# HGRN sample outputs with the query as 32-column stationary operand, norm squares in column groups and row scales from 128 rows, in a two-layer retention and HGRN2 step

## The reference

```python
# HGRN2, one sample token (b) and head (h); state S is 128 x 128
S_new = diag(f) @ S + outer(1 - f, i)
o     = S_new.T @ q
on    = o * rsqrt(mean(o*o) + 1e-6) * norm_g          # over the 128 values of a head
out   = (silu(g) * on) @ w_out
# retention, per head of 512 values
on    = (o - mean(o)) * rsqrt(var(o) + 1e-5) * gn_g
```

## Time and profile before

| | us |
|---|---|
| median of 3 runs | 1637.79 (1637.14 to 1643.33) |
| profiled execution | 1640.53, span 1638.7 |
| TensorE busy in the span | 1597.8 |
| VectorE busy | 621.6 |
| ScalarE busy | 421.6 |
| GpSimd busy | 79.4 |

### The profile page before, as it was taken

How to read it: one execution, slowest core, us unless ns; L and a number is a source line. 1 busy time by engine, 2 the same in 40 slices (tenths; PEclk the granted TensorE clock), 3 DMA queues, 4 the chain that set the end, 5 groups by cost and what they waited for, 6 DMA issues and landing times.

```text
span 1638.7 us, 32102 instructions
## 1 busy us (share of the span) xinstructions
PE 1597.8 (98%) x14348; PEld 955.6 (58%) x14348; DVE 621.6 (38%) x934; ACT 421.6 (26%) x606; POOL 79.4 (5%) x106
## 2 busy tenths in 40 slices
PE   7999999999999999999999999999999999999997
PEld 7888887999999999873333333333333333333333
DVE  6566576566655889543011100100111001001114
ACT  4444544444455575631001000010010000100001
POOL 1122221000000011001000000000000000000001
PEclk9999999999999999998999999999999999999999
DMA  9678879546455455267999999999999999999994
GB/s 337 223 270 294 296 259 383 168 155 197 132 179 192 164 167 168 96 260 298 398 411 393 423 417 391 420 417 388 420 383 422 416 385 422 417 389 421 403 404 191
DMA packets 138232, 514.93 MB, mean 314 GB/s; under 512 B 6700, under 2 KB 61172, under 8 KB 129780
## 3 DMA queue, kind: packets, MB, share of 16 engines
q1 hardware_dynamic: 117780, 447.93, 70.6%
q0 software_dynamic: 15824, 57.97, 10.1%
q10 hardware_dynamic: 4496, 7.02, 1.3%
HBM read 472.43 MB, written 40.47 MB: 313 GB/s over the span
## 4 chain that ended last, share of the span: by engine, by line
PE 86%; DVE 6%; DMA 2%; issue 1%; ACT 1%; POOL 0%; DVEq 0%; ACTq 0%
PE ps L1879 84%; DMA ring<-in_moe_w_up 2%; DVE ring_low_parts L1317 1%; DVE ring L1366 1%; PE ps L2025 1%; DMA ring<-in_state_retention 1%; ACT ring_low_parts L965 1%; DVE ring L1620 0%; DVE ring L1592 0%; DVE arena L1544 0%; DVE ring L1593 0%; ACT ring L1088 0%; DVE expert_arena L1846 0%; PE ps L2129 0%; DVE expert_arena L1836 0%
## 5 line engine op out<-in xcount | busy, mean ns | idle before, releaser
L1879 PE MATMUL ps<-ring,expert_x_turned 128*32 128x448 f32 x5376 | 510.0, 540 | 2.2 <-DMA ring<-in_moe_w_up 2.2
L1879 PEld LDWEIGHTS ps<-ring,expert_x_turned 128*32 128x32 f32 x5376 | 175.9, 110 | 333.7 <-issue 333.7
L1879 PE MATMUL ps<-normed_high,ring_low_parts 128*128 128x264 f32 x1344 | 268.8, 291 | 6.9 <-DVE arena L1312 3.0
L1879 PE MATMUL ps<-ring,expert_hidden_turned 128*32 128x512 f32 x2496 | 269.3, 592 | 0.0
L965 ACT CAST ring_low_parts<-ring 128x1024 fp32r<-128x1024 f32 (+2 forms) x180 | 180.0, 1001 | 245.9 <-PE ps L1879 241.6
L1317 DVE TENSOR_TENSOR ring_low_parts<-ring,ring_low_parts 128x1024 fp32r<-128x1024 f32 (+2 forms) x180 | 208.0, 1163 | 81.2 <-ACT ring_low_parts L965 81.2
L1879 PEld LDWEIGHTS ps<-normed_high,ring_low_parts 128*128 128x128 f32 x1344 | 218.4, 191 | 8.7 <-issue 3.6
L1811 DVE TENSOR_TENSOR expert_arena<-expert_arena,ps 128x1344 f32<-128x1344 f32 x16 | 24.9, 1554 | 510.8 <-PE ps L1879 510.8
L1879 PEld LDWEIGHTS ps<-ring,expert_hidden_turned 128*32 128x32 f32 x2496 | 83.3, 110 | 183.7 <-issue 183.4
L1879 PE MATMUL ps<-normed_low,ring_low_parts 128*128 128x264 f32 x640 | 161.6, 287 | 0.0
L1879 PE MATMUL ps<-h_parts,ring_low_parts 128*128 128x264 f32 x1056 | 130.0, 285 | 0.2 <-DVE h_parts L1301 0.2
(11 more groups left out here) (285 smaller groups left out, 1250.8 us busy)
## 6 DMA issues: line engine op xcount, KB each, us to landing
ring<-in_moe_w_gate SPq DMA_DIRECT2D x64, 1792.0 KB, 18.4
ring<-in_moe_w_down SPq DMA_DIRECT2D x48, 2048.0 KB, 22.7
ring<-in_moe_w_up SPq DMA_DIRECT2D x48, 1792.0 KB, 19.4
expert_piece_slot<-in_moe_w_up SPq DMA_DIRECT2D x16, 1792.0 KB, 19.9
ring<-in_ret_w_in SPq DMA_DIRECT2D x8, 2048.0 KB, 12.5
ring<-in_state_retention POOLq DMA_DIRECT2D x32, 512.0 KB, 7.8
out_ret_s<-ring POOLq DMA_DIRECT2D x32, 512.0 KB, 4.9
ring<-in_hg_w_in SPq DMA_DIRECT2D x8, 2048.0 KB, 8.2
```

What stands on the lines that cost most here:

```text
L1879: return nc.tensor.matmul(out, lhsT, rhs, start=first, stop=last)
```

## The change

The sample outputs of head t-2 exchange their operands: the query of a sample is the stationary operand, as one column of a 128x32 block that is otherwise zero, and the updated state is the moving one, with 128 columns. The outputs are rows now. Sample b goes to column group b % 4 (partitions 32c to 32c+31 of the bank), row b // 4. The padded queries (`hq_pad`, two buffers) are cleared once by GpSimd and filled by one VectorE copy per head ahead of `update_head`. ScalarE copies 128 columns instead of 8 to `s_rows`. After tile 10 a new step, `sample_rows`, turns the rows back: 8 matmuls, one for each head, with the rows of a head (128x128) as stationary operand and `hsel` (8 columns) as moving one, into a new group `("srow", 0)` in bank 0; ScalarE copies it out at t = 11.

The sums of squares go to partitions 32 (h % 4) of their bank: in retention each head in its own column group, in HGRN heads in turn over the four groups. Root and reciprocal run over 128 partitions, and the selecting matrix `rowsel` has 128 rows, zero but for one.

```diff
-    put("col_hg", np.broadcast_to(np.eye(8) / P, (P, 8, 8)).astype(f))
-    put("rowsel", np.broadcast_to(np.eye(8)[:, :, None], (8, 8, P)).astype(f))
+    put("col_hg", np.broadcast_to(np.eye(2, 32) / P, (P, 2, 32)).astype(f))
+    for j in range(8):
+        hs[32 * (j % 4) + j // 4, j] = 1
+        rs[32 * (j % 4) + j // 4, j] = 1
...
+        if t == 10:
+            add((("srow", 0), 0))
...  # GpSimd, after the retention layer
+            nc.gpsimd.memset(hq_pad, 0.0).then_inc(hq_zero, 1)
...  # ScalarE
-                        d = A.copy(oH[:, t - 2, NP_:NT], o[:, 256:264])
+                        d = A.copy(s_rows[:, t - 2, :], o[:, 256:384])
                     frees(d, ("itr", t - 1))
+                if t == 11:
+                    filled(act, ("srow", 0))
+                    frees(A.copy(oH[:, :, NP_:NT], bank(("srow", 0))[:, 0:64].rearrange("p (h b) -> p h b", h=8)), ("srow", 0))
...
-                    freed(act, ("itr", 8))
+                    freed(act, ("srow", 0))
...
-                    frees(A.activation(std8, bank(("hvar", 0), 8)[:, 0:NT], ACT.Sqrt, bias=eps_n[0:8]), ("hvar", 0))
+                    frees(A.activation(std8, bank(("hvar", 0))[:, 0:NT], ACT.Sqrt, bias=eps_n), ("hvar", 0))
...  # VectorE
                 if 1 <= t <= 8:
+                    if t >= 3:
+                        filled(dve, ("itr", t - 2))
+                    else:
+                        dve.wait_ge(hq_zero, 1)
+                    V.tensor_copy(hq_pad[:, (t - 1) % 2, :, 0], hq[:, t - 1, NP_:NT]).then_inc(hq_pad_ok, 1)
                     update_head(t - 1)
...  # TensorE, retention
-                    i = mm(bank(("var", 0), 8)[:, 0:NT], col_gn[:, h, :], square_of(h, e), h + e == 0, h + e == 6)
+                    i = mm(ps[32 * h:32 * h + 32, FILL[("var", 0)][0], 0:NT], col_gn[:, 0, :], square_of(h, e), e == 0, e == 3)
...
-                close(mm(bank(("rs", h))[:, 0:NT], rowsel[0:8, h, :], rstd[0:8, :]), ("rs", h))
+                close(mm(bank(("rs", h))[:, 0:NT], rowsel[:, h, :], rstd[:, :]), ("rs", h))
...  # TensorE, rows_of_i
                     freed(pe, ("ib", 1, h - 1))
+                    pe.wait_ge(hq_pad_ok, h)
+                    q = hq_pad[:, (h - 1) % 2, :, :].rearrange("p b n -> p (b n)")
                     for b in range(NS):
-                        i = mm(o[:, 256 + b:257 + b], hunit[(h - 1) % HUNITS][:, b, :], hq[:, h - 1, NP_ + b:NP_ + b + 1])
+                        c, a = b % 4, 32 * b - b // 4
+                        i = mm(ps[32 * c:32 * c + 32, FILL[("itr", h)][0], 256:384], q[:, a:a + 32],
+                               hunit[(h - 1) % HUNITS][:, b, :], b < 4, b >= 4)
                 close(i, ("itr", h))
+
+            def sample_rows():
+
+                freed(pe, ("itr", 8))
+                claim(("srow", 0))
+                for h in range(HH):
+                    i = mm(bank(("srow", 0))[:, NS * h:NS * h + NS], s_rows[:, h, :], cc("hsel"))
+                close(i, ("srow", 0))
...  # head_squares
-                    i = mm(bank(("hvar", 0), 8)[:, 0:NT], col_hg[:, h, :], osq[:, h, :], h == 0, h == 7)
+                    c = h % 4
+                    i = mm(ps[32 * c:32 * c + 32, FILL[("hvar", 0)][0], 0:NT], col_hg[:, h // 4, :], osq[:, h, :], h < 4, h >= 4)
...  # the loop over t
                 if 1 <= t <= 9:
                     rows_of_i(t)
+                if t == 10:
+                    sample_rows()
...
-                close(mm(bank(("hrs", h))[:, 0:NT], rowsel[0:8, h, :], rstd8), ("hrs", h))
+                close(mm(bank(("hrs", h))[:, 0:NT], rowsel[:, h, :], rstd8), ("hrs", h))
```

More of the change, by code:

```diff
@@ L422, in hybrid_step @@
         table_mark = part(small, 318, 2)
-        std8 = arena[0:8, 13568:13568 + NT]
-        rstd8 = arena[0:8, 13568 + NT:13568 + 2 * NT]
+        std8 = arena[:, 13568:13568 + NT]
+        rstd8 = arena[:, 13568 + NT:13568 + 2 * NT]
+        hq_pad = part(ring, spare + 1024, 2, 8, 32)
+        s_rows = part(arena, 6336 + 1088, 8, P)
         oH = hk
@@ L1046, in _ @@
             filled(act, ("var", 0))
-            frees(A.activation(std[0:8, :], bank(("var", 0), 8)[:, 0:NT], ACT.Sqrt, bias=eps_g[0:8]), ("var", 0))
+            frees(A.activation(std[:, :], bank(("var", 0))[:, 0:NT], ACT.Sqrt, bias=eps_g), ("var", 0))
             for h in range(RH):
@@ L1468, in _ @@
             freed(dve, ("var", 0))
[L1469 removed]
+            V.reciprocal(rstd[:, :], std[:, :]).then_inc(r8_ok, 1)
             for h in range(RH + 1):
```

15 lines of the change are left out of this document (10 added, 5 removed).

## The result

| | before | after |
|---|---|---|
| median of 6 runs each, us | 1637.47 (1636.08 to 1643.33) | 1628.70 (1627.38 to 1630.80) |
| profiled execution, span, us | 1640.53, 1638.7 | 1628.0, 1626.2 |

The ratio is 0.9943 (95% interval 0.9924 to 0.9963). The kernel became 8.8 us faster; the forecast was 1.0 us and its range ended at 1632.5. The profiled spans lie 12.5 us apart, more than the medians, because the profiled run of before was one of its slower ones. Three executions of two later kernels ran at a granted clock of 0.742 to 0.849 and took 1815 to 2058 us; they are left out of all medians here. First the page of after, then what answers to the rows of before.

The account below looks back on a forecast made before the run. More than half the span is the expert loop, paced by TensorE. Terms: +1.1 tile 10, -2.5+0.2 squares, -0.3 retention, +0.5 clock = -1.0, giving 1639.5 us profiled, 1636.8 on the median; range 1632.5 to 1642.5.

Parts of the forecast that it names:

- no gain is larger than the shift: Expert stage: a shift ahead of it is handed on one for one, and gains cannot exceed that shift.
- Sample outputs, TensorE: HGRN sample matmuls: 1.70 us a head becomes 0.8, saving 7.2 in all; tiling-mode drains could make the sum 0.6 worse.
- What VectorE lets through: 583 to 657 us: 3.6 us of cast waits recovered, less added copies; VectorE 2.8 us earlier, bounds 0 and 4.1.
- Tile 10: sample_rows waits for VectorE's scaling, TensorE idles some 3 us; product 8 starts 1.1 later, a clock fall adds 1.7.
- Norm squares: HGRN squares over four column groups: 3.65 us becomes 1.1, saving 2.5, with 0.2 given back.
- Retention: Retention norm squares, a head's four matmuls in one column group: 0.3 us saved, bounds 0 and 0.7.
- The clock behind the scale matmuls: After the HGRN scale matmuls the 6.5 us fall to 0.50 goes, worth 1.2 us, bounds 0 and 2.7.
- The clock elsewhere: Other clock falls: the one at 641.2 us worth nothing either way, the one at 265.8 going only in a rival.
- the end does not follow the start: Sign of a wrong prediction: the expert stage's start moves and its end does not move with it.
- A: Column groups do not overlap at 128 columns or drains eat it, leaving the tile 10 claim: +6, 1644 us; chance 0.2.
- B: Clock falls at 696 and 265.8 us both go and no new one comes: -4.4, 1633.4 us; chance 0.15.
- C: TensorE's saving counts in full because VectorE's order is looser: -8.3, 1629.5 us; chance 0.05.

Follow-up runs that it names:

- norm part alone: Kernel before with only the changed norms (column-group squares, 128-partition roots, 128-row scales), sample outputs as before, the eight new constant columns kept: 1621.95 us.
- rows in bank 2: Changed kernel with sample_rows put in bank 2 instead of bank 0, so it need not wait for the scaling of tile 10: 1621.78 us.
- same pair at 37376: The norm part alone and the changed kernel with rows in bank 2, both with the ring at byte 37376: 1623.65 and 1620.30 us.
- before shifted: Kernel before with two more keep_busy matmuls of 512 columns ahead of the routing stage: 1638.31 us.
- sample part alone: Kernel before with only the new sample outputs (padded queries, column groups, sample_rows at tile 10), norms made as before: 1633.19 us.
- retention norm alone: Kernel before with only the retention norm changed, HGRN norm and sample outputs as before, ring unmoved: 1636.16 us.

## Why the prediction was wrong, point by point

**The step that failed.** The prediction took the change to consist of its instructions alone: "no gain is larger than the shift" ahead of the experts, and no term at all for the eight new constants of `hsel`. They move the ring of weights, and that is worth 7.1 us in the changed kernel (1635.76 without, 1628.70 with). Without it the time lies inside the range of 1632.5 to 1642.5. Two more terms were wrong and hide each other: the fall of the clock at tile 10, and the falls behind 702 us.

**Sample outputs, TensorE: right.** 0.7 us a head, forecast 0.8. The Trainium skill's rule on changing the tiling mode (TensorEngine Tiling (Array Packing), Key Properties) says that each change drains TensorE. By the 228 ns of a record of 264 columns, four records of 128 columns one after another take 0.44 us; that is an estimate of the streaming alone, with the four groups fully overlapped. The 0.58 us to the next start leave 0.14 for the change behind, and 0.1 stands ahead: about 0.25 us for both, not the 0.3 each that would have made the sum worse. (The 0.50 of the prediction was half of a row that held such a change itself, so it was not streaming alone.)

**What VectorE lets through: right.** The waits for the cast went from 4.1 to 0.4 us (forecast 3.6 recovered). Where the claim was out of the way, the scale matmuls started 4.3 us earlier than in the norm part alone (683.12 against 687.43). But the two profiles were already 1.0 us apart at the reciprocal ahead of the HGRN layer, first with the rows in bank 2, then the norm part alone:

```profile
519.60 1.80 DVE L1324 RECIPROCAL rstd<-std 128x264 f32<-128x264 f32 x1 [1.71 <-ACT std L969]
```

```profile
520.60 1.80 DVE L1319 RECIPROCAL rstd<-std 128x264 f32<-128x264 f32 x1 [1.72 <-ACT std L967]
```

So 3.3 us belong to the sample outputs, and the same pair at 37376 gives 3.3 as well (4.69 less 1.43). The forecast was 2.8, with bounds 0 and 4.1.

**Tile 10: the mechanism was right, the term mis-sized.** It was claimed that TensorE would idle some 3 us for the scaling (3.90) and that the clock would fall (it did). The sum had 1.1 for the start of product 8 and 1.7 for the clock, 2.8 in all. Measured against the norm part alone, product 8 starts 2.3 later (657.77 against 655.45) and takes 2.6 more (6.22 for 3.6): 4.95 us, and the squares start 4.98 later. What was mis-sized is the fall: it was to be 3.4 us long, like the one at 641; it was 10.3 us, and took in `sample_rows` as well (1.65 us of the 2.3). Its length is a matter of the run: with the same wait it was 6.8 us in the changed kernel with the ring moved on, where the squares start 3.9 us later than in the norm part with the ring not moved (686.44 against 682.57). By medians the whole sample part cost 6.7 us beside the norm part, 5.8 with the ring at a slow place, and 3.1 beside the old norms (1633.19 against 1630.04).

**Norm squares: right.** 1.10 us, and from the first square to the scale matmuls 9.68 us became 6.96: 2.7 saved, forecast 2.5 less 0.2. **Retention: low.** Forecast 0.3 of a bound of 0.7; in the profile of the kernel with that norm alone the reciprocal starts 0.6 us earlier (258.05 for 258.64). That is one pair of profiles; in kernels whose retention norm is that of before the start lies anywhere from 258.64 to 260.54 at this place of the ring, later where the clock had fallen near 220 us.

**The clock behind the scale matmuls: the fall went, and was worth what was said.** In the kernels with 8 rows the fall behind them is there each time, 6.8 us long (before, before shifted, before with the ring moved, sample part alone, retention norm alone). In the twelve with 128 rows it is gone in ten, and two have one of 3.4 us up to 8 us behind (after with the ring moved, norm part with the ring at 36928). From the first output tile to the selection it takes 39.23 us after and 40.18 before: 0.95 us, forecast 1.2. That 128 rows in place of 8 take it away is shown by the kernel that changes only this, as far as one profile can; it is worth no more than 1.5 us in the median. In retention the same swap did not take the fall away: behind the scale matmuls from 8 rows there were 6.8 us at the lower clock in five profiles and 3.4 in one, behind those from 128 rows 6.8 in five, 3.4 in five and none in one.

**The clock elsewhere: a missed term.** The sum went through the falls at 265, 641 and 696 us and stopped at 702. The longest of all, 17.1 us at 0.50 in the routing, was in the same trace, at 736.6 to 753.7. The prediction treated everything behind the HGRN layer as one block that is shifted. It is not one: in the 17 profiles the way from selection to experts takes 8.9 us with no fall, 10.4 to 10.6 with one of 3.4, 11.7 with one of 6.8, and 15.3 and 16.6 with those of 13.7 and 17.1. By all runs the norm part lowers what the clock withholds from 19.5 to 9.3 us (ring unmoved). Over 99 runs of before the time follows the clock: 51 runs with a mean granted clock of 0.988 or more had a median of 1634.8 us, the 48 others 1642.1. So the norm part's 8.6 us are about 3.3 from the instructions (2.7 and 0.6, each from one pair of profiles), and the rest goes with a higher granted clock. This account does not close: 3.3 and 10.2 make 13.5, 4.9 more than the 8.6, and of these 3.2 went into longer waits for weights in the profile. Why the runs of the norm part meet fewer falls is open. Of the ten kernels with both new norms eight have no fall in the routing of their profile, of the seven others one has none; but each norm alone does not do it (6.8 us with the HGRN norm, none with the retention norm), and filling ahead brings a fall back.

**"No gain is larger than the shift", the term that put the time out of the range.** This rule failed on the ring. The eight constants of `hsel` have no term in the prediction; the line of the diff that adds them was

```diff
-               ... ("col_gn", 64), ("col_hg", 64), ("rowsel", 8 * P),
+               ... ("col_gn", 64), ("col_hg", 64), ("hsel", NS), ("rowsel", 8 * P),
```

They move every buffer behind the constants by 32 bytes, the ring of weights among them, onto a multiple of 256, and that alone is worth 8.4 us in the kernel before: 4.1 us in the rest behind the experts' start (884.75 to 880.7 in the profiles), the other part ahead of it, where most of it goes with the clock. In the changed kernel's profile the stage starts 8.4 us earlier and the span ends 12.5 us earlier; that the end does not follow the start was one of the prediction's own signs of being wrong. The reverse holds too: with a slow ring an earlier start is not handed on one for one (11.3 us became 8.3), because the lead of the transfers was used up, as the growth from 10.4 to 28.3 us in the earlier trace rows said. I read that row as support for the rule, but it spoke against it.

**The rivals.** A (1644) fell with the overlap. B had the falls at 696 and 265.8 go; the first did, the second stayed, 6.8 us long. C gave 1629.5, close to the result and for another reason: TensorE's saving did not count in full, it was eaten at tile 10. The sum as forecast, ring aside, is answered by the changed kernel with the ring moved on: 2.8 us below before, forecast 1.0, interval 0.9969 to 1.0006. Two misses of opposite sign hide in it, the wait at tile 10 (worse than forecast by some 3 us) and the norm part (better by 5).

## What to carry to other kernels

A new constant or buffer moves all that is allocated behind it: compute where the buffers that transfers fill begin before and after, and compare the GB/s of a stretch ahead of anything that changed. Go through every stretch at the lower clock up to the end of the span, not to the end of the stage that is edited; here the length of one such stretch behind the edit differed between kernels by more than the edited instructions saved. A group that is put into a bank plan costs what its claim waits for, and the cheapest repair is another bank: one digit gave 6.9 us here.

## What the runs showed of the hardware

- The rate of the transfers from DRAM into the ring in SBUF hangs on the place of the ring: 410 to 411 GB/s against 384 to 386 between 16 and 40 us, 412 to 414 against 406 to 408 beside the experts, over all kernels. Beginnings on 36864 and 37376 were fast; 36832, 36896, 36928 and 36992 were slow.
- Four column groups overlap nearly fully at 128 moving columns (16 float32 records in 0.58 us, 0.44 by an estimate from 228 ns for 264 columns), and at 264 columns with the heads in turn (16 records in 1.10 us for 3.65). A change into this layout and back cost about 0.25 us together.
- In the three kernels in which TensorE waited 3.9 us at tile 10 the granted clock fell to the lower level during the wait or just behind it, for 10.3, 6.8 and 6.8 us; the eight HGRN scale matmuls from 8 rows without a gap were followed by a fall of 6.8 us in all five profiles that have them, the same matmuls from 128 rows had one behind them, of 3.4 us, in two of twelve. In retention the same swap showed no such difference.
- The time of the unchanged kernel spreads over 1629.4 to 1646.6 us with the mean granted clock (0.984 to 0.993), so a profile of one run shows one sample of where the falls lie.
